# Second feed-forward stage of a two-block transformer kernel: six of its eight 512-feature chunks by seven products of quarters

## The chip, the cores and the metric

The kernel runs on one core of a Trainium2 chip. The time is the device time of one execution in microseconds (us); a comparison uses the median of several executions.

## The reference, cut to what matters

The reference is two transformer blocks in float32 over 512 tokens of width 1024. The first block has two layers: latent attention with a feed-forward stage, then sliding-window attention with a feed-forward stage. The second block has a SwiGLU stage, a dilated attention with pooling, and another SwiGLU stage. What matters here is the feed-forward stage of layer i = 1 and its input:

```python
def modulate(x, g, shift, scale):
    return rmsnorm(x, g) * (1.0 + scale[:, None, :]) + shift[:, None, :]
...
h = modulate(x, g_mlp[i], sh2, sc2)                               # x, h: (1, 512, 1024)
y = jnp.square(jax.nn.relu(h @ w_ff1[i])) @ w_ff2[i]              # 1024 -> 4096 -> 1024
x = x + gt2[:, None, :] * y
```

## The kernel before, in words

Everything is kept transposed: a tile has 128 features on the partitions and the 512 tokens along the row. Every float32 product is made of three matmuls (`mm3`): each operand is split into a rounded high part and the low rest, and high x high, high x low and low x high are summed in PSUM. ScalarE makes the high part of a weight (`act_hi`), VectorE the low part (`dve_lo`), and the same two engines make the parts of the activations.

**Weights.** `PLAN` and `WT` list all weights in the order of use. A weight of 1024 KB (128 partitions x 2048 elements) goes by a DMA of SyncE into one of three `RAW` buffers; its parts go into `WHI` and `WLO`, which have room for three such weights, or for six tiles of 1024 elements (names `UH`, `UL`). `AHEAD[w]` is the last weight that can be prepared while w is in use; `act_split` and `dve_split` prepare up to a given one. Both engines work through one list each, in the order in which the code was written: whatever stands ahead is done first.

**A feed-forward stage** (`pe_ff`, `act_ff`, `dve_ff`) has four blocks q of 1024 hidden features. The up-projection of block q + 1 stands ahead of the down-projection of block q. A chunk of 512 features takes two weights, 96 matmuls of 512 columns. Of the first chunk the tokens come in two halves of 256 columns (`halves`). A hidden tile goes PSUM, ReLU on ScalarE, square on VectorE, high part on ScalarE, low part on VectorE (`act_up`, `dve_up`). A down-projection is added to `X` by VectorE (`dve_resid`, `dve_add_x`). The stage begins with an opening (`act_opening`, `dve_opening`) that finishes the normalization of its input, and the last down-projection of a stage carries the sums of squares for the next one.

**The SwiGLU stages** (`pe_glu`, `act_glu`, `dve_glu`) already have both forms. Their first 768 features are computed plainly (`pe_gate`), the other 2048 in chunks of 512 by `pe_unit`. A unit takes seven products, m = 0 to 6, of a 512 x 256 quarter of weights (or a sum of quarters) and 256 tokens (or a sum of quarters of h). A product is 2 x 4 x 3 = 24 matmuls of 256 columns, so a unit has 168. It uses three PSUM banks: x, y and z. Between products, partial results are copied out (`act_keep`) and joined with later ones (`dve_join`). TensorE waits in the code for three things of these: product 2 waits until product 0's result was copied (`copied, (u, 1)`), product 3 until product 1's was, product 4 until product 2's was. VectorE makes the sums of weight quarters (`dve_sum`, products 1 to 4) and the four sums of h (`dve_t_sum`), which are made once for a stage and split by `act_t_hi` and `dve_t_lo`. In `dve_lo_seven` the sum for tile m + 1 is made just ahead of the low part of tile m. For the sums of h the stage keeps its h before the split in `H32`.

The rows of the profile name the helper lines: L66 matmul, L72 activation, L75 tensor_tensor, L83 scalar_tensor_tensor, L101 dma_start. In the ordinary chunks of the second feed-forward stage a row "DVE L75 128x2048 fp32r" is a low part of a weight; in a unit "DVE L75 t<-t,PS 128x512" is a join.

Of the kernel before, what the change touches and what calls it, by code (L numbers as in the profile page):

```python
# [4 lines left out]
S = 512  # L5
# [141 lines left out]
def bass_two_blocks(nc, A, out):  # L147
    ctx = ExitStack()
    with ctx:
# [352 lines left out]
        def count(name):  # L502
# [1169 lines left out]
        def norm_of(N, T, gain, shift, mods, h_free, before):  # L1672
# [10 lines left out]
        n_glu1 = norm_of("glu1", ("down", 1, 3), lambda j: G2[:, j:j + 1], None, [(misc, "g2")],  # L1683
                         lambda hf: [(acc, (("up", 1, 3, 1), 3, F))], [(acc, ("sum", "ff1", 1))])
        n_mix = norm_of("mix", ("w2", 1, 3), lambda j: col("mix_norm", j), None, [],
# [3 lines left out]
        n_end = norm_of("end", ("w2", 2, 3), None, None, [], None, [(acc, ("used", WX["s2"][-1] + 6))])  # L1689
        n_glu1.update(h32=H32[0])  # L1690
        n_glu2.update(h32=H32[1])

# [596 lines left out]
        def g_unit(i, c, gate):  # L2289
            return WX[f"s{i}"][2 * (c - 2) + gate]  # L2290

# [16 lines left out]
        def quarter_h(buf, r, t):  # L2308
            return buf[:, 4 * r:4 * r + 4, 256 * t:256 * t + 256]

        def dve_t_sum(e, i, n, N):
            h = H32[i - 1]
            e.wait_ge(hmul, (N, 7, 1))
            if n == 1:
                e.tensor_tensor(TL32[0][:, :, :], quarter_h(h, 0, 1), quarter_h(h, 0, 0), ALU.subtract).then_inc(
                    t_sum, (i, 1))
            elif n == 2:
                e.wait_ge(t_sum, (i, 1))
                e.tensor_tensor(TL32[1][:, :, :], quarter_h(h, 1, 1), TL32[0][:, :, :], ALU.subtract).then_inc(
                    t_sum, (i, 2))  # L2320
            else:
                if i == 1:
                    e.wait_ge(x_up, ("first", 7))
                e.tensor_tensor(TL32[2][:, :, :], quarter_h(h, 1, 1), quarter_h(h, 0, 1), ALU.subtract).then_inc(
                    t_sum, (i, 3))
                b21 = quarter_h(h, 1, 0)
                e.wait_ge(t_sum, (i, 2))
                e.wait_ge(h_lo, (N, 6, 0))
                e.wait_ge(h_lo_pool, (N, 7, 0))
                e.tensor_tensor(b21, b21, TL32[1][:, :, :], ALU.subtract).then_inc(t_sum, (i, 4))  # L2330

        def act_t_hi(e, i, n):
            if n < 4:
                e.wait_ge(t_sum, (i, n))
                e.activation(TH[n - 1][:, :, :], TL32[n - 1][:, :, :], ACT.Copy).then_inc(t_hi, (i, n))
            else:
                e.wait_ge(t_sum, (i, 4))
                e.wait_ge(acc, ("used", g_ws(i, 2)[1]))
                e.activation(quarter_h(HHI, 0, 1), quarter_h(H32[i - 1], 1, 0), ACT.Copy).then_inc(t_hi, (i, 4))

        def dve_t_lo(e, i, n):
            e.wait_ge(t_hi, (i, n))
            if n == 1:
                e.wait_ge(t_sum, (i, 2))
            if n == 2:
                e.wait_ge(t_sum, (i, 4))
            if n < 4:
                e.tensor_tensor(TL[n - 1][:, :, :], TL32[n - 1][:, :, :], TH[n - 1][:, :, :].bitcast(F32),
                                ALU.subtract).then_inc(t_lo, (i, n))
            else:  # L2350
                e.tensor_tensor(quarter_h(HLO, 0, 1), quarter_h(H32[i - 1], 1, 0), quarter_h(HHI, 0, 1).bitcast(F32),
                                ALU.subtract).then_inc(t_lo, (i, 4))
# [62 lines left out]
        def pe_unit(e, i, c, gate, nm):  # L2415
# [21 lines left out]
            def of_h(r, t):  # L2437
                for k in range(4 * r, 4 * r + 4):
                    e.wait_ge(h_hi, (nm["N"], k, t))
                    e.wait_ge(h_lo_pool if k % 2 else h_lo, (nm["N"], k, t))  # L2440
                return quarter_h(HHI, r, t), quarter_h(HLO, r, t)
# [84 lines left out]
        def dve_low(e, u, q):  # L2526
            i, c, gate = u
            if gate:
# [5 lines left out]
        def dve_unit(e, i, c, gate, nm):  # L2534
            u, w0 = (i, c, gate), g_unit(i, c, gate)
            dve_split(e, AHEAD[w0] - 1)
            dve_split(e, AHEAD[w0 + 1] - 1)
            dve_split(e, AHEAD[w0 + 2] - 1)
            dve_split(e, AHEAD[w0 + 3] - 1)
# [12 lines left out]
            dve_low(e, u, Q22)  # L2552
            dve_low(e, u, Q11)
            dve_times(e, u, Q21)
            dve_low(e, u, Q21)

# [91 lines left out]
        def pool_glu_norm(e, nm):  # L2648
            pool_normed(e, nm, 0, UPPER)
            pool_normed(e, nm, 1, ALL)  # L2650


# [595 lines left out]
        def pe_program(e):  # L3248
# [5 lines left out]
            pe_swa(e)  # L3254
            pe_ff(e, 1, n_ff1, n_glu1)
            pe_glu(e, 1, n_glu1, n_mix)
# [4 lines left out]
        def act_program(e):  # L3261
# [7 lines left out]
            act_swa(e)  # L3269
            act_ff(e, 1, n_ff1, n_glu1)  # L3270
            act_glu(e, 1, n_glu1, n_mix)
# [4 lines left out]
        def dve_program(e):  # L3276
# [6 lines left out]
            dve_swa(e)  # L3283
            dve_ff(e, 1, n_ff1, n_glu1, lambda j, h: (x_up, ("so", j, h)))
            dve_glu(e, 1, n_glu1, n_mix, lambda j, h: (x_up, ("first", j)))
# [125 lines left out]
```

## Time and profile before

| | |
|---|---|
| median of 3 executions | 2292.75 us (2289.44 to 2293.8) |
| the profiled execution | 2297.01 us, span of its instructions 2295.2 us |
| TensorE matmul busy | 2209.9 us, 96% of the span |
| VectorE busy | 1363.3 us, 59% |
| ScalarE busy | 916.4 us, 40% |
| GpSimd busy | 180.7 us, 8% |
| mean granted TensorE clock | 0.983 of full speed |
| second feed-forward stage | about 829 to 1188 us from the start of the span |

Busy times are unions of intervals on an engine; a matmul's end is modelled, and its own duration (hundreds of ns) overlaps its neighbours. The rate of TensorE is therefore read from how far apart the results of equal pieces of work arrive on the other engines.

### The profile page before, as it was taken

Reading aid. Unit: us, or ns where it says so; the run is one execution under the profiler, and the core shown is the slowest. Engines: PE = TensorE matmul, PEld = TensorE weight load, DVE = VectorE, ACT = ScalarE, POOL = GpSimd, SP = SyncE. Lnnn points to the kernel's source line nnn. Section 1 sums busy time; section 2 is a strip of 40 time slices with the busy share of each in tenths; the row PEclk is TensorE's granted clock in tenths of the full one; section 3 lists DMA queues with packets and bytes.
Section 4 is the critical chain, followed back from the end, with each engine's and each line's share of the span. In section 5 each row is a group of like instructions: output and inputs, shape, how many; then the busy total and the mean of one; then the engine's idle time right before and its main releaser. Section 6 shows DMA issues by size and latency. Waiting matters only on the chain.

```text
span 2295.2 us, 30850 instructions
## 1 busy us (share of the span) xinstructions
PE 2209.9 (96%) x12811; PEld 1930.2 (84%) x12811; DVE 1363.3 (59%) x2069; ACT 916.4 (40%) x1377; POOL 180.7 (8%) x155
## 2 busy tenths in 40 slices
PE   5989999999999899999999999999999999999998
PEld 3877888888898798888898999997878889899997
DVE  5677566556576664343356667754564545666674
ACT  3556343223255643232243444434443333433442
POOL 7220000000032100000020000002012001000000
PEclk8999999999999999999999999999999999999999
DMA  6442244555430213322312333333211332133230
GB/s 232 142 140 83 92 155 176 184 184 203 173 108 20 74 56 113 107 92 92 103 64 70 105 102 102 102 101 109 64 38 66 115 104 74 65 120 101 94 117 38
DMA packets 127728, 245.64 MB, mean 107 GB/s; under 512 B 4763, under 2 KB 36854, under 8 KB 127462
## 3 DMA queue, kind: packets, MB, share of 16 engines
q1 hardware_dynamic: 122832, 228.02, 29.4%
q0 software_dynamic: 4096, 15.28, 2.0%
q8 instruction: 102, 1.67, 0.3%
q10 hardware_dynamic: 662, 0.37, 0.1%
q14 instruction: 36, 0.29, 0.0%
HBM read 241.56 MB, written 2.10 MB: 106 GB/s over the span
## 4 chain that ended last, share of the span: by engine, by line
PE 83%; DVE 9%; ACT 3%; DMA 2%; issue 2%; POOL 0%; SPq 0%; DVEq 0%; ACTq 0%
PE PS L66 82%; DVE t L75 4%; ACT t L72 3%; DVE t L83 2%; DVE t L86 1%; DMA t<-in_ffn_w_dram 1%; PE PS L69 1%; DMA t<-in_w_ada_dram 1%; DVE t L79 0%; POOL t L75 0%; DVE t L92 0%; DVE t L80 0%; SPq L101 0%; DVE t L95 0%; DVEq L58 0%
## 5 line engine op out<-in xcount | busy, mean ns | idle before, releaser
L66 PE MATMUL PS<-t,t 128*128 128x256 f32 (+3 forms) x12444 | 2159.5, 337 | 54.0 <-ACT t L72 15.2
L66 PEld LDWEIGHTS PS<-t,t 128*128 128x128 f32 (+1 forms) x12444 | 1885.9, 190 | 324.7 <-issue 60.6
L72 ACT ACTIVATE t<-t 128x2048 fp32r<-128x2048 f32 (+8 forms) x663 | 605.9, 930 | 1000.8 <-DVE t L75 410.5
L75 DVE TENSOR_TENSOR t<-t,t 128x512 fp32r<-128x512 f32 (+9 forms) x640 | 730.4, 1155 | 450.1 <-ACT t L72 427.8
L72 ACT ACTIVATE t<-PS 128x512 f32<-128x512 f32 (+4 forms) x331 | 177.5, 551 | 244.1 <-PE PS L66 181.2
L75 POOL TENSOR_TENSOR t<-t,t 128x512 f32<-128x512 f32 (+2 forms) x71 | 86.6, 1220 | 1125.6 <-ACT t L72 952.3
L75 DVE TENSOR_TENSOR t<-t,PS 128x512 f32<-128x512 f32 (+2 forms) x116 | 70.9, 616 | 139.8 <-PE PS L66 134.3
L83 DVE SCALAR_TENSOR_TENSOR t<-t,t,t 128x1024 f32<-128x1024 f32 (+2 forms) x149 | 139.9, 943 | 16.8 <-DMA t<-in_w_ada_dram 11.1
L72 ACT ACTIVATE t<-t,t 128x256 fp32r<-128x256 f32 (+5 forms) x212 | 112.4, 537 | 91.1 <-DVE t L83 46.0
L83 DVE SCALAR_TENSOR_TENSOR t<-PS,t,t 128x512 f32<-128x512 f32 (+3 forms) x120 | 76.8, 642 | 95.7 <-PE PS L66 85.7
L75 DVE TENSOR_TENSOR t<-t 128x512 f32<-128x512 f32 (+4 forms) x119 | 80.9, 680 | 23.7 <-ACT t L72 23.0
L69 PE MATMUL PS<-t,t 128*128 128x128 f32 (+1 forms) x367 | 60.0, 305 | 27.0 <-DMA t<-in_x_dram 6.9
L83 DVE SCALAR_TENSOR_TENSOR t<-PS,t 128x512 f32<-128x512 f32 (+1 forms) x84 | 49.3, 610 | 53.5 <-PE PS L66 53.5
L69 PEld LDWEIGHTS PS<-t,t 128*128 128x128 f32 (+1 forms) x367 | 46.5, 155 | 35.8 <-issue 10.6
L83 DVE SCALAR_TENSOR_TENSOR t<-t,t,PS 128x256 f32<-128x256 f32 (+1 forms) x133 | 60.9, 487 | 20.6 <-PE PS L66 17.1
L79 DVE TENSOR_SCALAR t<-t,t 128x128 f32<-128x128 f32 (+5 forms) x159 | 56.7, 389 | 5.4 <-DMA t<-in_w_ada_dram 3.1
L79 POOL TENSOR_SCALAR t<-t 128x512 f32<-128x512 f32 x28 | 48.9, 1748 | 73.5 <-DVE t L86 49.2
L86 DVE CUSTOM_DVE_ANT_0 t<-PS,t 128x128 f32<-128x128 f32 (+1 forms) x112 | 38.4, 352 | 20.7 <-PE PS L66 20.6
L75 DVE TENSOR_TENSOR t<-PS,t 128x512 fp32r<-128x512 f32 (+2 forms) x40 | 24.9, 634 | 34.1 <-ACT t L72 24.2
L101 POOL DMA_DIRECT2D t<-in_k_dist_dram x1 | 0.5, 543 | 426.3 <-PE PS L66 426.3
L72 ACT ACTIVATE t<-PS,t 128x2 f32<-128x2 f32 (+3 forms) x44 | 19.0, 432 | 29.9 <-PE PS L66 29.2
L86 DVE CUSTOM_DVE_ANT_0 t<-PS,t,t 128x384 f32<-128x384 f32 (+3 forms) x56 | 29.2, 522 | 2.0
(30 smaller groups left out, 154.1 us busy)
## 6 DMA issues: line engine op xcount, KB each, us to landing
t<-in_w_ff_dram SPq DMA_DIRECT2D x64, 1024.0 KB, 5.2
t<-in_ffn_w_dram SPq DMA_DIRECT2D x60, 1024.0 KB, 4.9
t<-in_w_ada_dram SPq DMA_DIRECT2D x36, 1024.0 KB, 5.6
t<-in_w_in_dram SPq DMA_DIRECT2D x13, 1024.0 KB, 4.9
t<-in_w_ada_dram POOLq DMA_DIRECT2D x24, 512.0 KB, 4.3
t<-in_swa_w_qkv_dram SPq DMA_DIRECT2D x6, 1024.0 KB, 5.4
t<-in_ffn_w_dram SPq DMA_DIRECT2D x8, 768.0 KB, 4.4
t<-in_w_in_dram SPq DMA_DIRECT2D x24, 256.0 KB, 3.7
```

The lines of the kernel that those rows point to most:

```text
L66: return Instr(self.real and self.real.matmul(o, lhs, rhs, start=start, stop=stop, **more))
L69: return Instr(self.real and self.real.transpose(o, src, ident))
L72: return Instr(self.real and self.real.activation(o, src, func, **more))
L75: return Instr(self.real and self.real.tensor_tensor(o, a, b, op))
L79: return Instr(self.real and self.real.tensor_scalar(o, a, s1, s2, op0))
L83: return Instr(self.real and self.real.scalar_tensor_tensor(o, a, s, b, op0, op1))
L86: return Instr(self.real and self.real.tensor_tensor_reduce(**more))
L101: return Instr(self.real and self.real.dma_start(o, src))
```

## The change

The second feed-forward stage gets functions of its own, `pe_ff1`, `act_ff1` and `dve_ff1`. Of its 4096 hidden features the first 1024 (chunks c = 0 and 1) are computed plainly, the other six chunks (c = 2 to 7) by `pe_unit`. The order on TensorE is: chunks 0 and 1, unit 2, down-projection 0, units 3 and 4, down 1, units 5 and 6, down 2, unit 7, down 3. A down-projection q uses chunks 2q and 2q + 1. The unit's activation becomes three operations of ScalarE on each quarter of 128 x 512 (ReLU, square, high part); VectorE makes the low parts, two of the four of a unit later than before (`dve_late`). Since this stage's h has a shift (`sh2`), two of the four sums of h add it when they are split, as four pieces of 256 columns each. h before the split goes to `H32[0]`. The four sums of h and their parts are made while chunks 0 and 1 are computed. Parts of the diff (the pure renaming of `H32` indices and the calls in the four programs are left out):

```diff
+        def ff1_plan():
+            w1, w2 = wt(A["w_ff1"][1]), wt(A["w_ff2"][1])
+            square("up1", w1)
+            for q, chunks in enumerate(FUNITS):
+                for c in chunks:
+                    unit("s0", w1, 512 * c)
+                square("down1", w2, k0=8 * q)
+
+        FUNITS = ((2,), (3, 4), (5, 6), (7,))
...
         def act_t_hi(e, i, n):
             if n < 4:
                 e.wait_ge(t_sum, (i, n))
+                if i == 0 and n > 1:
+                    for k in range(4):
+                        e.activation(TH[n - 1][:, k, :], TL32[n - 1][:, k, :], ACT.Identity, bias=t_shift(n, k)).then_inc(
+                            t_hi, (i, n))
+                    return
...
-            e.activation(quarter_of(GL32[s], q), src, ACT.Silu).then_inc(relu, (u, q))
+            g = quarter_of(GL32[s], q)
+            if i:
+                e.activation(g, src, ACT.Silu).then_inc(relu, (u, q))
+                return
+            e.activation(g, src, ACT.Relu).then_inc(relu, (u, q))
+            e.wait_ge(relu, (u, q))
+            e.activation(g, g, ACT.Square).then_inc(squared, (u, q))
+            e.wait_ge(squared, (u, q))
+            e.activation(quarter_of(GH[s], q), g, ACT.Copy).then_inc(hid_hi, (u, q))
...
+        def act_ff1(e, nm, nxt):
+            ws = WX["up1"]
+            act_opening(e, nm, ws[0:2])
+            act_step(e, ws[0])
+            act_up1(e, 0, 0)
+            act_up1(e, 0, 1)
+            act_step(e, ws[2])
+            act_t_hi(e, 0, 1)
+            act_t_hi(e, 0, 2)
+            act_step(e, ws[3])
+            act_t_hi(e, 0, 3)
+            act_up1(e, 1, F)
+            for q in range(4):
+                for c in FUNITS[q]:
+                    act_unit(e, 0, c, 0)
...
+        def dve_ff1(e, nm, nxt, before):
+            ws = WX["up1"]
+            dve_opening(e, nm, ws[0:2])
+            dve_step(e, ws[0])
+            dve_up1(e, 0, 0)
+            dve_t_sum(e, 0, 1, "ff1")
+            dve_t_sum(e, 0, 2, "ff1")
+            dve_up1(e, 0, 1)
+            dve_step(e, ws[2])
+            dve_t_sum(e, 0, 3, "ff1")
+            dve_t_lo(e, 0, 1)
+            dve_t_lo(e, 0, 2)
+            dve_step(e, ws[3])
+            dve_t_lo(e, 0, 3)
+            dve_up1(e, 1, F)
+            for q in range(4):
+                late = None
+                for c in FUNITS[q]:
+                    dve_unit(e, 0, c, 0, nm, late)
+                    late = (0, c, 0)
+                dve_late(e, late)
```

**Place A, ScalarE between the first chunk and unit 2.** Before, ScalarE comes from the last tiles of chunk 0 (`t_125<-`, the high parts), makes the high parts of three weights and goes on with the four tiles of chunk 1 (`<-PS 128x512` is the ReLU, then the high part):

```order
L72 ACTIVATE t_125<-t_61 128x256
L72 ACTIVATE t_54<-t_51 128x2048
L72 ACTIVATE t_52<-t_49 128x2048
L72 ACTIVATE t_53<-t_50 128x2048
L72 ACTIVATE t_62<-PS 128x512
L72 ACTIVATE t_125<-t_62 128x512
L72 ACTIVATE t_63<-PS 128x512
```

Now, at the same place (t_150 to t_155 are the unit's weight tiles, t_163 to t_165 the sums that VectorE made for them, t_141 to t_143 the high parts of the sums of h, which are t_147 to t_149):

```order
L72 ACTIVATE t_130<-t_61 128x256
L72 ACTIVATE t_54<-t_51 128x2048
L72 ACTIVATE t_150<-t_49 128x1024
L72 ACTIVATE t_151<-t_163 128x1024
L72 ACTIVATE t_141<-t_147 128x1024
L72 ACTIVATE t_142<-t_148,t_78 128x256 x4
L72 ACTIVATE t_152<-t_164 128x1024
L72 ACTIVATE t_153<-t_165 128x1024
L72 ACTIVATE t_143<-t_149,t_82 128x256 x4
L72 ACTIVATE t_62<-PS 128x512
L72 ACTIVATE t_131<-t_62 128x512
```

Four weight tiles and three sums of h stand ahead of the first ReLU of chunk 1. And behind the last tile of chunk 1 the list goes on with tile m = 4 and then with the copy of product 0 of unit 2 (`t_63<-PS`), tile 5, and the copies of products 1 and 2:

```order
L72 ACTIVATE t_62<-PS 128x512
L72 ACTIVATE t_131<-t_62 128x512
L72 ACTIVATE t_154<-t_166 128x1024
L72 ACTIVATE t_63<-PS 128x512
L72 ACTIVATE t_155<-t_50 128x1024
L72 ACTIVATE t_61<-PS 128x512
L72 ACTIVATE t_62<-PS 128x512
```

The copy of product 0 moved behind all of chunk 1's tiles.

**Place B, VectorE over the same stretch,** from the second sum of h to the third. It begins behind the tiles of chunk 0's second half; t_57 is the low part of the fourth plain weight, t_156 to t_158 those of tiles 0 to 2:

```order
L75 TENSOR_TENSOR t_57<-t_51,t_54 128x2048
L75 TENSOR_TENSOR t_163<-t_49,t_50 128x1024
L75 TENSOR_TENSOR t_156<-t_49,t_150 128x1024
L75 TENSOR_TENSOR t_82<-t_78 128x4
L75 TENSOR_TENSOR t_149<-t_138 128x1024
L75 TENSOR_TENSOR t_138<-t_138,t_148 128x4x256
L75 TENSOR_TENSOR t_144<-t_147,t_141 128x1024
L83 SCALAR_TENSOR_TENSOR t_145<-t_148,t_78,t_142 128x256 x4
L75 TENSOR_TENSOR t_164<-t_163,t_49 128x1024
L75 TENSOR_TENSOR t_157<-t_163,t_151 128x1024
L75 TENSOR_TENSOR t_165<-t_50,t_164 128x1024
L75 TENSOR_TENSOR t_158<-t_164,t_152 128x1024
```

Before, two low parts of plain weights stood here and nothing else.

**Place C, ScalarE at the end of unit 2** (the same in unit 7). t_62, t_61 and t_63 are the joined quarters; t_53 is the high part of the first weight of the down-projection that follows the unit:

```order
L72 ACTIVATE t_135<-t_62 128x2x256
L72 ACTIVATE t_135<-t_135 128x2x256
L72 ACTIVATE t_129<-t_135 128x2x256
L72 ACTIVATE t_135<-t_61 128x2x256
L72 ACTIVATE t_135<-t_135 128x2x256
L72 ACTIVATE t_129<-t_135 128x2x256
L72 ACTIVATE t_53<-t_51 128x2048
L72 ACTIVATE t_135<-t_63 128x2x256
```

That weight stands behind two quarters of three operations each.

## Rows read from the trace of the kernel before

**Rows 1.** The page: span, TensorE's busy time, and the chain that ended last.

```profile
span 2295.2 us, 30850 instructions
...
PE 2209.9 (96%) x12811; PEld 1930.2 (84%) x12811; DVE 1363.3 (59%) x2069; ACT 916.4 (40%) x1377; POOL 180.7 (8%) x155
...
PE 83%; DVE 9%; ACT 3%; DMA 2%; issue 2%; POOL 0%; SPq 0%; DVEq 0%; ACTq 0%
```

**Rows 2.** Timeline of TensorE: start, us, instruction, count, idle before and its releaser.

```profile
849.68 339.29 PE L66 MATMUL PS<-t,t 128*128 128x256 f32 x1628 [1.43 <-ACT t L72]
```

**Rows 3.** Timeline of VectorE, plain chunks: low parts of every second weight.

```profile
935.30 2.29 DVE L75 TENSOR_TENSOR t<-t,t 128x2048 fp32r<-128x2048 f32 x1 [6.71 <-ACT t L72]
...
957.06 2.29 DVE L75 TENSOR_TENSOR t<-t,t 128x2048 fp32r<-128x2048 f32 x1 [8.59 <-ACT t L72]
```

**Rows 4.** Timeline of VectorE in a unit of the first SwiGLU stage: two joins.

```profile
1345.06 0.69 DVE L75 TENSOR_TENSOR t<-t,PS 128x512 f32<-128x512 f32 x1 [5.84 <-PE PS L66]
...
1347.94 0.69 DVE L75 TENSOR_TENSOR t<-t,PS 128x512 f32<-128x512 f32 x1 [1.05 <-PE PS L66]
```

**Rows 5.** Timeline of VectorE, chunk 0 and chunk 1 of the second feed-forward stage.

```profile
851.87 0.43 DVE L75 TENSOR_TENSOR t<-t,t 128x256 fp32r<-128x256 f32 x1 [0.48 <-ACT t L72]
...
853.12 0.43 DVE L75 TENSOR_TENSOR t<-t,t 128x256 fp32r<-128x256 f32 x1 [0.48 <-ACT t L72]
853.46 0.42 DVE L75 TENSOR_TENSOR t<-t 128x256 f32<-128x256 f32 x1
...
872.23 0.68 DVE L75 TENSOR_TENSOR t<-t 128x512 f32<-128x512 f32 x1
...
874.22 0.68 DVE L75 TENSOR_TENSOR t<-t 128x512 f32<-128x512 f32 x1
```

**Rows 6.** Timeline of ScalarE, last tile of chunk 0, two tiles and last tile of chunk 1.

```profile
857.16 0.38 ACT L72 ACTIVATE t<-PS 128x256 f32<-128x256 f32 x1
...
872.95 0.63 ACT L72 ACTIVATE t<-t 128x512 fp32r<-128x512 f32 x1 [1.56 <-DVE t L75]
...
878.95 0.60 ACT L72 ACTIVATE t<-PS 128x512 f32<-128x512 f32 x1 [0.73 <-DVE t L75]
```

**Rows 7.** Groups of instructions by form, whole run: count, busy us, mean ns, idle before.

```profile
L75 DVE TENSOR_TENSOR t<-t,t 128x2048 fp32r<-128x2048 f32 x127 | 290.9, 2296 | 275.9 <-ACT t L72 275.8
L72 ACT ACTIVATE t<-t 128x2048 fp32r<-128x2048 f32 x127 | 241.6, 1909 | 382.3 <-PE PS L66 380.0 <-DMA t<-in_mla_w_ukv_dram 1.9
L75 DVE TENSOR_TENSOR t<-t,t 128x1024 fp32r<-128x1024 f32 x122 | 148.6, 1222 | 25.2 <-ACT t L72 21.1
L72 ACT ACTIVATE t<-t 128x1024 fp32r<-128x1024 f32 x122 | 128.4, 1056 | 146.7 <-DVE t L75 146.5
L83 DVE SCALAR_TENSOR_TENSOR t<-t,t,t 128x256 fp32r<-128x256 f32 x64 | 31.9, 499 | 4.0 <-ACT t L72 4.0
L72 ACT ACTIVATE t<-t,t 128x256 fp32r<-128x256 f32 x64 | 31.4, 507 | 46.0 <-DVE t L83 46.0
```

**Rows 8.** Timeline of ScalarE in a SwiGLU unit: quarters taken after a join.

```profile
1345.78 2.44 ACT L72 ACTIVATE t<-t 128x512 f32<-128x512 f32 x2 [2.06 <-DVE t L75]
```

**Rows 9.** Timeline of TensorE: one of its longest idle stretches inside the program.

```profile
215.25 3.54 PE L66 MATMUL PS<-t,t 128*128 128x1 f32 x16 [3.90 <-DVE t L83]
```

**Rows 10.** Windows: PE, PEld, DVE, ACT, POOL busy, then PEclk, DMA share, GB/s.

```profile
215.00:222.00 7.00, 6.75 (x28) 6.27 (x29) 3.24 (x7) 1.97 (x4) 0.00 (x0) 0.52 0.00 0
...
1603.00:1611.00 8.00, 5.83 (x27) 4.36 (x28) 5.09 (x7) 4.44 (x7) 2.30 (x2) 1.00 0.34 98
```

**Rows 11.** Timeline of VectorE where two SwiGLU units stand behind each other.

```profile
1469.91 2.36 DVE L75 TENSOR_TENSOR t<-t,t 128x1024 f32<-128x1024 f32 x2 [2.27 <-DMA t<-in_ffn_w_dram]
1472.19 0.68 DVE L75 TENSOR_TENSOR t<-t,PS 128x512 f32<-128x512 f32 x1
```

**Rows 12.** Timeline of ScalarE, same stretch: product 2 copied, then the next unit's product 0.

```profile
1467.24 0.60 ACT L72 ACTIVATE t<-PS 128x512 f32<-128x512 f32 x1 [0.85 <-PE PS L66]
...
1482.04 0.60 ACT L72 ACTIVATE t<-PS 128x512 f32<-128x512 f32 x1 [0.82 <-PE PS L66]
```

More of the change, by code:

```diff
@@ L526, in bass_two_blocks @@
         misc, misc_act, misc_pool = count("small_dve"), count("small_act"), count("small_pool")
+        squared = count("squared_act")
         summed, t_sum, t_hi, t_lo, joined = (count(n) for n in (
@@ L2346, in dve_t_lo @@
                 e.wait_ge(t_sum, (i, 4))
-            if n < 4:
+            if i == 0 and n in (2, 3):
+                for k in range(4):
+                    e.scalar_tensor_tensor(TL[n - 1][:, k, :], TL32[n - 1][:, k, :], t_shift(n, k),
+                                           TH[n - 1][:, k, :].bitcast(F32), ALU.add, ALU.subtract).then_inc(t_lo, (i, n))
+            elif n < 4:
                 e.tensor_tensor(TL[n - 1][:, :, :], TL32[n - 1][:, :, :], TH[n - 1][:, :, :].bitcast(F32),
@@ L2439, in of_h @@
                     e.wait_ge(h_hi, (nm["N"], k, t))
[L2440 removed]
+                    e.wait_ge(h_lo_pool if nm["shift"] is None and k % 2 else h_lo, (nm["N"], k, t))
                 return quarter_h(HHI, r, t), quarter_h(HLO, r, t)
@@ L2532, in dve_low, with dve_late, dve_unit @@
                                 ALU.subtract).then_inc(hid_lo, (u, q))
-        def dve_unit(e, i, c, gate, nm):
+        def dve_late(e, u):
+            dve_low(e, u, Q11)
+            dve_low(e, u, Q21)
+        def dve_unit(e, i, c, gate, nm, late=None):
             u, w0 = (i, c, gate), g_unit(i, c, gate)
@@ L2537, in dve_unit @@
             dve_split(e, AHEAD[w0 + 1] - 1)
+            if late:
+                dve_late(e, late)
             dve_split(e, AHEAD[w0 + 2] - 1)
@@ L2552, in dve_unit @@
             dve_low(e, u, Q22)
-            dve_low(e, u, Q11)
-            dve_times(e, u, Q21)
-            dve_low(e, u, Q21)
+            if i:
+                dve_low(e, u, Q11)
+                dve_times(e, u, Q21)
+                dve_low(e, u, Q21)
         def g_of(i, blk):
@@ L2650, in pool_glu_norm, with pe_up1, act_up1 @@
             pool_normed(e, nm, 1, ALL)
+        def pe_up1(e, c, nm):
+            tag = ("up", 1, c)
+            pe_linear(e, tag, WX["up1"][2 * c:2 * c + 2], FOUR, h_of(nm), lambda n, hf: (relu, (tag, n, hf)), halves=c == 0,
+                      mid=pe_open(e, nm) if c == 0 else None)
+        def act_up1(e, c, hf):
+            s = g_slot(0, c)
+            for n in range(4):
+                key = (("up", 1, c), n, hf)
+                ta.take(key, (hid_lo, key))
+                tm = TMP[ta[key]][:, COLS[hf]]
+                e.wait_ge(acc, key)
+                e.wait_for(ta.free(key))
+                e.activation(tm, PS[:, banks[key], COLS[hf]], ACT.Relu).then_inc(relu, key)
+                e.wait_ge(sqr, key)
+                e.activation(GH[s][:, n, COLS[hf]], tm, ACT.Copy).then_inc(hid_hi, key)
@@ new lines, in pe_ff1 @@
+        def pe_ff1(e, nm, nxt):
+            pe_up1(e, 0, nm)
+            pe_up1(e, 1, nm)
+            for q in range(4):
+                for c in FUNITS[q]:
+                    pe_unit(e, 0, c, 0, nm)
+                for n2 in range(2):
+                    last = q == 3 and n2 == 1
+                    pe_linear(e, (("down", 1, q), n2), down_ws(1, q, n2), FOUR, f_of(q), x_until(("down", 1, q), 4 * n2),
+                              halves=last, mid=pe_close(e, nxt) if last else None)
+        def act_ff1(e, nm, nxt):
[13 more added lines that the diff above has]
+                    act_unit(e, 0, c, 0)
+                for n2 in range(2):
+                    act_resid(e, ("down", 1, q), nxt if q == 3 else None, 4 * n2, down_ws(1, q, n2),
+                              halves=q == 3 and n2 == 1, weighted=True)
@@ new lines, in dve_ff1 @@
+        def dve_ff1(e, nm, nxt, before):
[13 more added lines that the diff above has]
+            dve_up1(e, 1, F)
+            for q in range(4):
+                late = None
+                for c in FUNITS[q]:
+                    dve_unit(e, 0, c, 0, nm, late)
+                    late = (0, c, 0)
+                dve_late(e, late)
+                for n2 in range(2):
+                    T = ("down", 1, q)
+                    dve_resid(e, T, nxt if q == 3 else None, (T, n2), 4 * n2, down_ws(1, q, n2),
+                              lambda j: MOD[:, 1, 40 + j:41 + j],
+                              before if q == 0 else lambda j, h: (x_up, (("down", 1, q - 1), j, h)), [(mod, (1, 5))],
+                              halves=q == 3 and n2 == 1)
```

63 lines of the change are left out of this document (46 added, 17 removed).

## The prediction

> **What bounds the kernel now.** I read the page first [rows 1]: TensorE is busy 96% of the span and has 83% of the chain that ended last. So a change is worth what it does to TensorE's work and to its waits. The timeline of TensorE comes next [rows 2]: from 849.68 us it runs 339 us without a gap, through nearly all of the stage that is changed. Every matmul less there is time gained, and every new wait is time lost. What a matmul costs I read from how far apart equal results arrive on other engines.
>
> **The matmuls.** In plain chunks VectorE makes a weight's low part in step with TensorE: a chunk (two weights, 96 matmuls of 512 columns) lasts 957.06 - 935.30 = 21.76 us, 226.7 ns for a matmul [rows 3]. In a unit the joins of products 3 and 4 are 1347.94 - 1345.06 = 2.88 us apart, 24 matmuls of 256 columns, 120 ns for one [rows 4]. Seven products are 20.16 us. A chunk saves 1.60 us; six save **9.6 us** (576 matmuls of 512 columns, 130.6 us, become 1008 of 256, 121.0 us). An eighth of the columns is saved, but 256 columns cost more than half of 512, so under a half of that eighth is left.
>
> The Trainium skill ("TensorE: Matmul & The Clock Gate", "Wait — 56ns, not 53.3ns?") gives a warm matmul as its columns at 2.4 GHz plus about 2.5 ns. By that the chunk would go from 20.7 to 18.3 us and the six would save 14.2 us. The rows above do not show these spacings for either size, so the sum uses the rows.
>
> **The opening: does ScalarE copy product 0 in time?** This is place A of the change. TensorE finishes chunk 0 at 857.1 (the last ReLU starts at 857.16) and chunk 1 at 878.9 (ReLU at 878.95) [rows 6]. Unit 2's products 0 and 1 then run to 878.9 + 5.76 = 884.7, and product 2 needs the copy of product 0. Before, ScalarE followed TensorE tile by tile. I carry the two lists forward from where they are as before, the end of chunk 0's first half on VectorE at 853.5 [rows 5], with the durations of [rows 7]: 1.2 us for a 1024-element operation of VectorE, 1.06 on ScalarE, 2.29 and 1.91 for 2048 elements, 0.40 to 0.50 for a 256-column piece.
> - VectorE: two sums of h, to 855.9. Four tiles of chunk 0's second half, 1.25 us apart [rows 5], to 861.0.
> - ScalarE: high part of the fourth plain weight, 860.5 to 862.4. VectorE: its low part, to 864.7. TensorE wants it at 857.1 + 10.9 = 868.0: no wait.
> - VectorE: weight sum 1, low part of tile 0, sums 3 and 4 of h, low part of sum 1 of h, five operations and a tiny one, to 870.5. Then four pieces, to 872.1. Then sum 2, low part 1, sum 3, low part 2 (to 876.9).
> - ScalarE, held back by those sums: tile 3 to 876.7, then sum 3 of h in four pieces to 878.3. VectorE: its low part, to 880.0.
> - Chunk 1's four tiles, which were ready from 868.0 + 2.7 = 870.7, start here. One takes 1.99 us (square to square) [rows 5], the high part comes 0.72 after the square [rows 6]. The last square is at 885.9, its high part ends at 887.2, its low part at 887.9.
> - VectorE: weight sum 4, to 889.1. ScalarE: tile 4, to 890.2, and only then the copy, **890.7**.
>
> Product 2 therefore waits 890.7 - 884.7 = **6.0 us**. Nothing hides this: TensorE has no other work in its list. Once it resumes, the later copies and tiles (3 at about 890.2, 4 at 891.4) are ready before their products. Beyond this place the sums of h cost nothing more: they are made once.
>
> **The clock after that wait.** After an idle 3.9 us [rows 9] the granted clock was 0.52 over the next 7 us [rows 10], its lower level of 1.2 GHz nearly throughout; after about 2.2 idle us in another stretch it stayed at 1.00. Six us are longer than both, so I expect the fall. Matmuls then take about 213 ns instead of 120 (256 columns at 1.2 GHz). The low stretch after the restart lasts between 4 and 7 us, which loses 44% of it, 1.8 to 3.1 us. I take **2.3**; no fall would be 0.
>
> **The first weight of the down-projection behind a single unit (place C).** Its high part stands behind the quarter of the second join. A quarter was one operation on ScalarE (0.63 us, with the 2048 high part 2.44 together, 0.72 behind the join [rows 4, 8]); now it is three, 2.0 us. From the join of product 4: 0.72 + 2.0 - 0.1 until the high part starts, + 1.9, + 2.3 for the low part is 6.8 us, while TensorE ends the unit 5.76 us after that join, or a little earlier by its own clock. That is a wait of 1.1 to 1.3 us behind unit 2 and behind unit 7, **2.4 together**. In the pairs the buffers fall the other way: the weight is prepared one product earlier, and nothing waits.
>
> **The pairs.** A unit needs 11 operations of 1024 elements (1.2 us), three joins and four low parts (0.69 us) from VectorE: 18.0 of 20.16 us. ScalarE has 7 x 1.06 + 3 x 0.6 + 4 x 2.0 = 17.2. Both fit, with a lead of several tiles from the down-projection, which asks two low parts and four additions of VectorE in 21.8 us. The tight point is again the copy of product 0 of the second unit. By the same bookkeeping it is done 1.8 us before it is wanted. Where two SwiGLU units stand behind each other, VectorE lost 2.27 us to a DMA [rows 11], and the next unit's product 0 came 14.80 us after product 2 instead of 14.40 [rows 12], so 0.4 us is what such a place cost. I take 0, with 0 to 0.8 for both pairs.
>
> DMA bytes do not change, nor do GpSimd's and SyncE's lists. More ReLU, square and copy on ScalarE in place of squares on VectorE costs nothing by itself. The handover to the SwiGLU stage keeps its instructions: 0.
>
> **Sum.** -9.6 + 6.0 + 2.3 + 2.4 = **+1.1 us**. Against the profiled execution (2297.0, which is 4.3 us or 0.2% above the median of the three) that is 2298.1; against the median of 2292.75 it is 2293.9, and this is what I predict. The bounds: with the 2.4 alone 2285.6; all costs at their upper end (6.0 + 1, 3.1, 2.6, 0.8) 2296.7. About 0.2%, 4.6 us, is what a measurement of this kernel can tell from no change.
>
> **Rivals.**
> - *The opening is not late.* If ScalarE or VectorE gets through the list 6 us sooner than I add up (the sums of h overlap waits that I count twice), the 6.0 and 2.3 go: -7.2, **2285.6**. For it: the SwiGLU stages hide the same sums of h without a wait at their first unit. Against it: they have three plain steps of 21.8 us for this, here there are two, and the list is short of 6 us, not of one. Half of it, a wait under 3 us with no fall of the clock, gives about -4.6 and decides whether it can be measured. Chance 0.22.
> - *The pairs run dry.* The takes of quarters Q11 and Q21 (four us of ScalarE together at the end of a unit) stand ahead of the next unit's first copy. If each of the twelve operations of a unit costs 0.15 us more than I take, or the DMA comes as late as in [rows 11], the margin of 1.8 us is gone. From there each us is paid on TensorE in both pairs, and the weight behind the pair comes late as well: 2 x (1.5 to 2.5) more, +4 to +6, so with the rest **2298 to 2300**, slower. Against it: the bookkeeping and the 0.4 us. Chance 0.13.
> - *Narrow matmuls cost half.* If 256 columns took half of 226.7 ns here, 113.4, the saving would be 16.3 us and the sum about -5: 2287.5. Joins 2.88 us apart speak against it. This is the place of the skill's rule above, by whose figures the sum would be -3.5. Chance 0.03.
> - *The change saves nothing in matmuls* because the units run at another rate: excluded by 168 against 96 in the code and [rows 3, 4].
>
> **How the numbers follow.** Forecast 0.62, not late 0.22, pairs 0.13, narrow 0.03. Two thirds of "not late" and the narrow case are faster by over 0.2%, and a tail of the forecast: 0.21. The pairs and a longer low clock are slower: 0.16. Within 0.2%: 0.63. The range reaches from the middle of "not late" to the pairs: 2285 to 2298.5.
>
> **What would show it.** In the profile after: a TensorE idle stretch of about 6 us some 56 us after the stage's start (near 885), released by ScalarE, and a granted clock near 0.5 behind it; idle stretches of about 1.2 us at the ends of units 2 and 7 released by VectorE; joins 2.88 us apart in the pairs; the stage's end about 1 us later than before. A gap under 3 us at 885 would make the forecast wrong towards faster; idle stretches at product 2 of units 4 and 6 towards slower.

## The result and the profile after

The changed kernel takes 2296.07 us (median, 2293.52 to 2300.51), the kernel before 2293.02 us beside it (2288.96 to 2297.56), 22 runs of each. The ratio is 1.0015, with a 95% interval of 1.0008 to 1.0021: the change costs 1.8 to 4.8 us. The median is inside the predicted range and 0.13% above the kernel before, less than the 0.2% that was named as the bound of "no change" (the upper end of the interval, 4.8 us, just passes it); the sign is the one of the sum.

The page of the changed kernel, the lines that answer to [rows 1]: 432 matmuls more, TensorE 5.9 us less busy, and the span 1.4 us longer all the same.

```profile
span 2296.6 us, 31886 instructions
...
PE 2204.0 (96%) x13243; PEld 1943.2 (85%) x13243; DVE 1415.2 (62%) x2132; ACT 965.9 (42%) x1459; POOL 179.3 (8%) x155
```

The timeline of TensorE over the changed stage, which answers to [rows 2] (start, us, instruction, count, then the idle time before it and what ended it):

```profile
847.39 35.00 PE L66 MATMUL PS<-t,t 128*128 128x256 f32 x204 [1.17 <-ACT t L72]
888.38 17.21 PE L66 MATMUL PS<-t,t 128*128 128x256 f32 x120 [6.00 <-ACT t L72]
906.79 231.66 PE L66 MATMUL PS<-t,t 128*128 128x512 f32 x1416 [1.20 <-issue]
1139.64 49.20 PE L66 MATMUL PS<-t,t 128*128 128x512 f32 x320 [1.20 <-issue]
1189.72 70.46 PE L66 MATMUL PS<-t,t 128*128 128x256 f32 x391 [0.88 <-DVE t L75]
```

Where one stretch of 339 us stood, there are four now. The first row is chunks 0 and 1 and unit 2's products 0 and 1; behind it TensorE waits 6.00 us for ScalarE. The two waits of 1.20 us stand behind unit 2 and behind unit 7. (The releaser reads "issue" and not VectorE, as the prediction had it. VectorE's low part of the weight begins at 904.40 and takes 2.29 us, so it ends 0.1 us before the restart; experiment 4 shows that this weight is what TensorE waits for.) Between 906.79 and the next wait, through both pairs, the view shows no gap.

I measure the stage from TensorE's restart at its head to its restart behind its end: before from 849.68 [rows 2] to 1189.84, now from 847.39 to 1189.72. The first of these ends is this row of the kernel before, from the same view:

```profile
1189.84 1.89 PE L66 MATMUL PS<-t,t 128*128 128x256 f32 x9 [0.88 <-DVE t L75]
```

So 340.16 us became 342.33, **+2.17 us**. This leaves out the opening ahead of the head, which the change touches too. The last point where both kernels still do the same is the start of a run of 370 matmuls, here in the kernel before and in the changed one:

```profile
780.23 53.70 PE L66 MATMUL PS<-t,t 128*64 128x128 f32 x370
...
778.92 53.70 PE L66 MATMUL PS<-t,t 128*64 128x128 f32 x370
```

From there to the head are 849.68 - 780.23 = 69.45 us before and 847.39 - 778.92 = 68.47 now. The opening became 0.98 us shorter, and it is 68.44 to 68.46 us in the other kernels below except that of experiment 2. VectorE and ScalarE finish a tile of h each 0.79 us there instead of each 0.91; that it comes from `H32[0]`, where h now has a place of its own, is likely and was not tested. So from the common point the change costs **+1.19 us**, and +2.17 from head to end.

A stage's length is steadier than the span. From a point of the SwiGLU stage (1464.00 us in the changed kernel) all kernels of this study have the same instructions, and yet the rest of their profiled runs lasted between 828 and 836 us, so a span can differ by some us with no edit at all.

ScalarE's timeline shows why product 2 waited. Chunk 1's last tile, tile m = 4, then the copy of product 0:

```profile
882.81 0.58 ACT L72 ACTIVATE t<-PS 128x512 f32<-128x512 f32 x1
...
886.79 1.06 ACT L72 ACTIVATE t<-t 128x1024 fp32r<-128x1024 f32 x1 [1.89 <-DVE t L75]
887.75 0.58 ACT L72 ACTIVATE t<-PS 128x512 f32<-128x512 f32 x1
```

The copy starts at 887.75, and product 2 at 888.38, which is 41.0 us behind the head of the stage; the bookkeeping had 890.7 - 849.7 = 41.0. It stands behind tiles that ScalarE shares with VectorE in turns, one each 1.99 us.

The clock in windows of 2 us (TensorE busy with its count, granted clock, DMA share, GB/s):

```profile
886.00:888.00 2.00, 0.00 (x0) 0.86 0.00 0
888.00:890.00 2.00, 1.62 (x7) 0.50 0.04 8
...
892.00:894.00 2.00, 2.00 (x11) 0.50 0.78 283
894.00:896.00 2.00, 2.00 (x18) 0.93 0.06 23
```

It falls while TensorE still waits and stays at half, 1.2 GHz, until about 894. The price comes from VectorE's timeline:

```profile
899.88 0.69 DVE L75 TENSOR_TENSOR t<-t,PS 128x512 f32<-128x512 f32 x1 [1.06 <-PE PS L66]
...
923.42 0.75 DVE L83 SCALAR_TENSOR_TENSOR t<-PS,t,t 128x512 f32<-128x512 f32 x1 [0.54 <-PE PS L66]
```

The first row is the join of product 4. It comes 899.88 - 888.38 = 11.50 us after product 2 began; in experiment 3, where the clock stays at 1.00, the same join comes 8.92 us after it (3 x 2.88 = 8.64, and 0.28 by which a join starts behind its product's end). So the fall cost **2.58 us**. The second row is one of the additions of a down-projection. The same addition of the next down-projection, two units later, is at 1007.28:

```profile
1007.28 0.75 DVE L83 SCALAR_TENSOR_TENSOR t<-PS,t,t 128x512 f32<-128x512 f32 x1 [0.53 <-PE PS L66]
```

The step is 83.86 us; a down-projection (192 matmuls at 226.7 ns) and two units of 20.16 us make 83.84. The pair costs nothing beyond its matmuls.

### The profile page after: what moved, and what is told of

Read it like the earlier page. It is cut to its first block, busy times and chain, and to the rows that moved or that the text cites. A ratio compares the mean times of both kernels' runs of the same rounds, so it can differ in the third digit from the quotient of the medians.

```text
span 2296.6 us, 31886 instructions
## 1 busy us (share of the span) xinstructions
PE 2204.0 (96%) x13243; PEld 1943.2 (85%) x13243; DVE 1415.2 (62%) x2132; ACT 965.9 (42%) x1459; POOL 179.3 (8%) x155
## 3 DMA queue, kind: packets, MB, share of 16 engines
q0 software_dynamic: 4096, 15.28, 2.0%
## 4 chain that ended last, share of the span: by engine, by line
PE 81%; DVE 10%; ACT 4%; DMA 2%; issue 2%; POOL 0%; SPq 0%; DVEq 0%; ACTq 0%
PE PS L66 80%; DVE t L75 5%; ACT t L72 4%; DVE t L83 3%; DVE t L86 1%; DMA t<-in_ffn_w_dram 1%; PE PS L69 1%; DMA t<-in_w_ada_dram 1%; DVE t L79 1%; POOL t L75 0%; DVE t L92 0%; DVE t L80 0%; SPq L101 0%; DVE t L95 0%; DVEq L58 0%
## 5 line engine op out<-in xcount | busy, mean ns | idle before, releaser
L66 PE MATMUL PS<-t,t 128*128 128x256 f32 (+4 forms) x12876 | 2152.7, 330 | 62.6 <-ACT t L72 20.9
L66 PEld LDWEIGHTS PS<-t,t 128*128 128x128 f32 (+2 forms) x12876 | 1898.4, 190 | 314.0 <-issue 63.0
L72 ACT ACTIVATE t<-t 128x512 f32<-128x512 f32 (+8 forms) x737 | 655.0, 905 | 954.0 <-DVE t L75 479.2
L75 DVE TENSOR_TENSOR t<-t,t 128x1024 fp32r<-128x1024 f32 (+9 forms) x692 | 776.3, 1138 | 395.4 <-ACT t L72 341.5
L75 DVE TENSOR_TENSOR t<-t,PS 128x512 f32<-128x512 f32 (+2 forms) x134 | 83.3, 626 | 157.3 <-PE PS L66 150.5
L83 DVE SCALAR_TENSOR_TENSOR t<-t,t,t 128x1024 f32<-128x1024 f32 (+2 forms) x157 | 144.8, 929 | 14.5 <-DMA t<-in_w_ada_dram 7.5
L75 DVE TENSOR_TENSOR t<-t 128x512 f32<-128x512 f32 (+4 forms) x104 | 74.2, 714 | 14.9 <-ACT t L72 14.5
L69 PEld LDWEIGHTS PS<-t,t 128*128 128x128 f32 (+1 forms) x367 | 46.9, 156 | 35.1 <-issue 10.4
```

Source lines behind the costliest of these rows:

```text
L66: return Instr(self.real and self.real.matmul(o, lhs, rhs, start=start, stop=stop, **more))
L69: return Instr(self.real and self.real.transpose(o, src, ident))
L72: return Instr(self.real and self.real.activation(o, src, func, **more))
L75: return Instr(self.real and self.real.tensor_tensor(o, a, b, op))
L83: return Instr(self.real and self.real.scalar_tensor_tensor(o, a, s, b, op0, op1))
```

## The experiments

None of them changes what the kernel computes. Each stage length is read from one profiled execution. Medians of the kernel before beside them: 2293.96 us (30 runs) for experiments 1 to 4, 2293.55 us (21 runs) for 5 and 6.

**1. All units in pairs, the first down-projection ahead of them.** Down-projection 0 needs chunks 0 and 1 alone, so it can come before the first unit. It gives ScalarE and VectorE 43.5 us in which TensorE needs little of them, and no unit stands alone in front of a down-projection.

```diff
-        FUNITS = ((2,), (3, 4), (5, 6), (7,))
+        FUNITS = ((), (2, 3), (4, 5), (6, 7))
...
-                dve_late(e, late)
+                if late:
+                    dve_late(e, late)
```

> The order of units becomes: chunks 0 and 1, down-projection 0, units 2 and 3, down 1, units 4 and 5, down 2, units 6 and 7, down 3. All the work stays. Theory: the waits come from where the units stand. The 6.0 us wait at product 2 of the first unit goes, because a down-projection of 43.5 us now lies between the sums of h and that unit; with it the stretch at the low clock (2.9 us) goes, and both waits of 1.2 us, since no unit stands alone. Against the changed kernel -11 us, about 2285; against the kernel before -8 to -9.5 us, ratio 0.996. Three pairs cost 0.1 to 0.4 us each. Rival (pairs run dry, or the sums of h cost the same elsewhere): an idle stretch of 2 us or more at product 2 of units 3, 5 or 7, or at the first down-projection, which takes chunk 1 late; then 2290 or more.

Measured: 2286.23 us (2278.54 to 2288.86, 7 runs), ratio to the kernel before 0.9963 (0.9949 to 0.9977), which is 5 to 12 us faster. TensorE's timeline:

```profile
845.45 330.27 PE L66 MATMUL PS<-t,t 128*128 128x256 f32 x2060 [1.16 <-ACT t L72]
1176.59 1.90 PE L66 MATMUL PS<-t,t 128*128 128x256 f32 x9 [0.88 <-DVE t L75]
```

The view shows no gap in the stage, which lasts 331.14 us: 11.19 less than in the changed kernel, 9.02 less than before. The three waits and the clock were 6.00 + 2.58 + 1.20 + 1.20 = 10.98. So nearly all that the changed kernel lost went with the place of the units. Of the 9.6 us that the matmuls should save 9.0 are seen. The rest stands in the first pair, here by the same addition of down-projections 0 and 1 on VectorE:

```profile
891.04 0.75 DVE L83 SCALAR_TENSOR_TENSOR t<-PS,t,t 128x512 f32<-128x512 f32 x1 [0.54 <-PE PS L66]
...
975.42 0.75 DVE L83 SCALAR_TENSOR_TENSOR t<-PS,t,t 128x512 f32<-128x512 f32 x1 [0.54 <-PE PS L66]
```

That step is 84.38 us, the next two are 83.86 each. The first pair alone loses 0.5 us, a little above the 0.1 to 0.4 expected for a pair; why was not traced. This kernel beats both others.

**2. The four sums of h on GpSimd.** At place B they are VectorE's, and they delay its weights and with them ScalarE's tiles.

```diff
-            dve_t_sum(e, 0, 1, "ff1")
-            dve_t_sum(e, 0, 2, "ff1")
...
-            dve_t_sum(e, 0, 3, "ff1")
...
+        def pool_t_sums(e):
+            for n in (1, 2, 3):
+                dve_t_sum(e, 0, n, "ff1")
```

> The four sums of h move from VectorE to GpSimd, which is idle there; nothing else is touched. Theory: VectorE's list ahead of chunk 1's tiles is what is late, so four operations of 1.2 us less there shorten the wait at product 2 of unit 2 by 4.9 us, from 6.0 to about 1.1, and an idle stretch of 1.1 us leaves the clock at full speed: another 2.9 us. Against the changed kernel -7 to -8 us, about 2288.5, a little faster than before (ratio 0.998). Rival (ScalarE's list, not VectorE's, sets it): the wait shortens by less than 2 us, the clock still falls, and the time stays within 2 us of the changed kernel's.

Measured: 2297.0 us (2293.78 to 2300.72, 12 runs), ratio 1.0015 (1.0006 to 1.0023): no better than the changed kernel. TensorE's timeline:

```profile
851.33 36.48 PE L66 MATMUL PS<-t,t 128*128 128x256 f32 x204 [5.98 <-ACT t L72]
891.02 16.15 PE L66 MATMUL PS<-t,t 128*128 128x256 f32 x120 [3.21 <-ACT t L72]
```

The wait at product 2 did shrink, from 6.00 to 3.21 us, but little of that is what was hoped for. The stage's first wait grew from 1.17 to 5.98 us, and the clock fell behind it (36.48 us for 204 matmuls that take 35.00), so TensorE itself came 1.48 us later to product 2. Counted from the head of the stage, product 2 starts at 891.02 - 851.33 = 39.69 us instead of 40.99: the two lists gained 1.30 us where 4.9 were expected. By its size that is the rival's answer (under 2 us). It is a lower bound of what the sums cost, since VectorE lost another 1.6 us behind the head (its low part at 851.04 took 2.02 us instead of 0.43). Counted from the common point ahead of the opening (778.05 here) the stage ends 2.45 us later than in the changed kernel. What happened stands in the timelines of GpSimd and VectorE, here in this order:

```profile
840.82 2.59 POOL L75 TENSOR_TENSOR t<-t 128x1024 f32<-128x1024 f32 x1 [79.70 <-DVE t L83]
843.49 2.44 POOL L75 TENSOR_TENSOR t<-t,t 128x1024 f32<-128x1024 f32 x1
845.88 4.39 POOL L75 TENSOR_TENSOR t<-t 128x1024 f32<-128x1024 f32 x1
```

```profile
841.31 2.38 DVE L83 SCALAR_TENSOR_TENSOR t<-t,t,t 128x256 fp32r<-128x256 f32 x1 [0.18 <-ACT t L72]
843.61 4.47 DVE L75 TENSOR_TENSOR t<-t,t 128x2048 fp32r<-128x2048 f32 x1
848.00 2.56 DVE L75 TENSOR_TENSOR t<-t 128x256 f32<-128x256 f32 x1
```

In the changed kernel the same three operations of VectorE take 0.48, 2.29 and 0.42 us. They alternate: VectorE's short one ends at 843.69, 0.3 us behind GpSimd's first sum; its long one is done 2.15 us behind GpSimd's second (845.93), as if it had run only then; GpSimd's third takes 4.39 instead of 2.44, over that same time; and VectorE's next ends at 850.56, 0.3 us behind that (850.27). One holds the other up for whole operations. The Trainium skill ("SBUF — State Buffer", "Who interferes with whom") has this as a rule: an operation of VectorE with two inputs in SBUF and one of GpSimd that reads SBUF exclude each other, and the one that comes second waits. The trace agrees, at both engines. So the sums still cost VectorE time, and at a place where it has none to spare.

**3. The wait filled with unused matmuls.** 44 matmuls of 256 columns into a free bank between products 1 and 2 of unit 2; their results are not used. The wait stays as long, but TensorE is busy in it.

```diff
+            if u == (0, 2, 0):
+                e.wait_for(banks.free((u, "z")))
+                for _ in range(44):
+                    e.matmul(PS[:, banks[u, "z"], 0:256], HHI[:, 4, 0:128], HHI[:, 4, 0:256], start=True, stop=True)
```

> 44 matmuls of 256 columns, whose results nobody uses, are put on TensorE between products 1 and 2 of unit 2, where it waits 6.0 us (44 x 0.12 = 5.3 us). Theory: the clock falls because TensorE is idle; filled, the wait still ends at the same moment, but product 2 and what follows run at full speed. The stretch at 0.50 in the windows behind it is gone, the join of product 3 comes 5.8 us after the wait's end instead of 8.6, and the time is 2.9 us less than the changed kernel's, equal to the kernel before (2293). Rival (the clock falls there anyway, or its fall is hidden under ScalarE's and VectorE's later steps): the same time as the changed kernel, 2296.

Measured: 2291.16 us (2289.6 to 2292.08, 11 runs), ratio 0.9991 (0.9982 to 0.9999). TensorE's timeline:

```profile
881.31 5.44 PE L66 MATMUL PS<-t 128*128 128x256 f32 x44
887.47 14.65 PE L66 MATMUL PS<-t,t 128*128 128x256 f32 x120 [0.71 <-ACT t L72]
```

VectorE's timeline, the join of product 4:

```profile
896.39 0.69 DVE L75 TENSOR_TENSOR t<-t,PS 128x512 f32<-128x512 f32 x1 [1.06 <-PE PS L66]
```

The windows at the place where the clock had been at half:

```profile
888.00:890.00 2.00, 2.00 (x19) 1.00 0.30 30
890.00:892.00 2.00, 2.00 (x19) 1.00 1.01 381
```

Product 2 starts 40.98 us behind the head of the stage (846.49), as in the changed kernel, so the wait is untouched. The clock stays at 1.00, and the stage lasts 339.70 us, 2.63 less. The join of product 4 comes 8.92 us after product 2's start instead of 11.50. Both give the term for the clock by itself, 2.6 us, and work that computes nothing was worth it. Against the changed kernel the median is 4.9 us lower; 2.6 of that is in the stage, and where the rest comes from is not shown.

**4. The down-projection's weight ahead of the quarter (place C).** In units 2 and 7 alone:

```diff
+            if u in ((0, 2, 0), (0, 7, 0)):
+                act_split(e, AHEAD[w0 + 6] - 1)
             act_take(e, u, Q22)
```

> In units 2 and 7 alone ScalarE makes the high part of the next down-projection's first weight ahead of the second quarter (Q22) instead of behind it. Theory: this order alone makes the two waits of 1.2 us at the ends of single units. The high part is then ready 1.65 us after the join of product 4, the low part stands behind the join of product 5 and ends 5.8 us after that of product 4, so 0.1 to 0.3 us of each wait is left. Against the changed kernel -2 us, near what can be measured; the idle stretches in the timeline decide. Rival (VectorE's lows or a late DMA hold the weight): both waits stay at 1.0 us or more.

Measured: 2296.52 us (2293.09 to 2298.95, 10 runs), ratio 1.0014 (1.0005 to 1.0023). TensorE's timeline:

```profile
883.94 16.64 PE L66 MATMUL PS<-t,t 128*128 128x256 f32 x120 [6.00 <-ACT t L72]
900.73 231.66 PE L66 MATMUL PS<-t,t 128*128 128x512 f32 x1416 [0.15 <-issue]
1132.54 49.21 PE L66 MATMUL PS<-t,t 128*128 128x512 f32 x320 [0.15 <-issue]
```

Both waits of 1.20 us are 0.15, from one operation moved past three, so place C is what the prediction took it for. The stage (842.95 to 1182.62, 339.67) is 2.66 us shorter. Of this 2.10 are the two waits. Most of the rest is not from this edit's place at all: behind the same wait of 6.00 us the 120 matmuls took 16.64 us instead of 17.21, because the clock had fallen earlier in the wait (0.50 from 882 on, 2 us ahead of the restart) and was back sooner. The medians do not show the gain: the two ratios differ by 0.0001, with intervals of about 1.5 and 2 us to either side, so a gain of 2.7 us is at the edge of what they allow. That the waits are gone is shown; that the time follows is not.

**5. The copy of product 0 two tiles earlier.** Is it ScalarE's order or the two engines' load that makes the 6.0 us?

```diff
                 e.activation(GH[s][:, n, COLS[hf]], tm, ACT.Copy).then_inc(hid_hi, key)
+                if (c, n) == (1, 1):
+                    act_keep(e, (0, 2, 0), 1, 0, "x", Q11, at=4)
```

> The changed kernel with one instruction of ScalarE moved: the copy of product 0 of unit 2 stands between the second and the third tile of chunk 1 instead of behind the fourth tile and tile m = 4 of the weights, and writes a buffer that is free there (same count of instructions, same work). Theory (it is the place of the copy in the list that makes the 6.0 us wait): product 0 ends near 879.5, the copy runs near 881, product 2 starts without a wait at 882.4 and ends at 885.3; product 3 then waits for the high and low part of its weight tile, made behind chunk 1's tiles at about 888, so 2.3 to 3 us; the clock may stay at 1.00 behind a wait that short; about -3.3 us against the changed kernel from the wait alone, -6.2 if the clock stays up as well. Rival (both engines are simply short of time up to this point, so the order makes no difference): the wait moves to product 3 in full, 6 us, and the time stays as that of the changed kernel.

Measured: 2295.79 us (2291.19 to 2298.59, 11 runs), ratio 1.0006 (0.9997 to 1.0015). TensorE's timeline and clock:

```profile
845.51 37.87 PE L66 MATMUL PS<-t,t 128*128 128x256 f32 x228 [1.16 <-ACT t L72]
887.80 13.28 PE L66 MATMUL PS<-t,t 128*128 128x256 f32 x96 [4.42 <-ACT t L72]
```

```profile
886.00:888.00 2.00, 0.20 (x1) 0.97 0.00 0
888.00:890.00 2.00, 2.00 (x10) 0.50 0.67 113
890.00:892.00 2.00, 2.00 (x14) 0.68 1.04 404
```

228 matmuls pass now before the wait: product 2 did not wait. But product 3 did, for 4.42 us. I had left the copy of product 1 out of the expectation; it starts at 887.17, behind tiles 4 and 5, and ends this wait. The clock fell all the same, which the expectation had left open. The stage lasts 339.65 us, 2.68 less: 1.6 from the shorter wait, and 1.0 because the fall cost 1.5 us here and not 2.6 (13.28 us for the 96 matmuls; with the clock up, in experiment 3, they take 14.65 - 2.88 = 11.77). So the order on ScalarE has a part in the 6.0 us, 1.6 of them by this one operation; whether the copy of product 1, moved as well, would gain more was not tried.

**6. One more ReLU on each quarter.** About 2.6 us more on ScalarE per unit, with the same result.

```diff
             e.activation(g, g, ACT.Square).then_inc(squared, (u, q))
             e.wait_ge(squared, (u, q))
+            e.activation(g, g, ACT.Relu).then_inc(again, (u, q))
+            e.wait_ge(again, (u, q))
```

> The changed kernel with one more ReLU on each quarter of all six units (the result is unchanged): about 0.65 us each, 2.6 us of ScalarE per unit, which takes it from 17.2 to 19.8 of a unit's 20.16 us. It asks how near the pairs are to running dry. Theory (margin 1.2 us before the copy of product 0 of a pair's second unit): two quarters stand ahead of that copy, +1.3 us, so the margin is just used up and TensorE waits 0 to 0.5 us there in each pair; behind units 2 and 7 two quarters stand ahead of the weight's high part, so these waits grow from 1.2 to about 2.5 us each; the stage becomes 2.6 to 3.6 us longer. Rival (the delay adds up from quarter to quarter through the buffers, as in the prediction's case of the pairs that run dry): TensorE waits 1.5 us or more in each pair and behind the pairs too, the stage 5 us or more longer.

Measured: 2300.95 us (2295.04 to 2304.02, 11 runs), ratio 1.0026 (1.0017 to 1.0035). TensorE's timeline:

```profile
887.92 17.19 PE L66 MATMUL PS<-t,t 128*128 128x256 f32 x120 [5.97 <-ACT t L72]
906.96 71.30 PE L66 MATMUL PS<-t,t 128*128 128x512 f32 x408 [1.85 <-issue]
978.55 84.11 PE L66 MATMUL PS<-t,t 128*128 128x256 f32 x528 [0.28 <-ACT t L72]
1063.57 78.35 PE L66 MATMUL PS<-t,t 128*128 128x256 f32 x480 [0.91 <-ACT t L72]
1143.77 49.20 PE L66 MATMUL PS<-t,t 128*128 128x512 f32 x320 [1.86 <-issue]
```

The margin of the pairs is used up as expected: there are waits of 0.28 and 0.91 us at product 2 of the second units. The second is above the 0 to 0.5 expected, and VectorE's timeline shows what differs there, a weight that came later by DMA:

```profile
962.04 2.36 DVE L75 TENSOR_TENSOR t<-t,t 128x1024 f32<-128x1024 f32 x2 [1.10 <-DMA t<-in_w_ff_dram]
...
1047.06 2.36 DVE L75 TENSOR_TENSOR t<-t,t 128x1024 f32<-128x1024 f32 x2 [1.72 <-DMA t<-in_w_ff_dram]
```

VectorE waited 0.62 us longer in the second pair, and TensorE 0.63. In the changed kernel these two waits are 1.22 and 1.09 us. The down-projections are now 84.40 and 85.01 us apart (additions at 925.19, 1009.59 and 1094.60) instead of 83.86, +0.5 and +1.2, and the 0.65 us of the quarters do not add up. The waits behind units 2 and 7 grew by 0.65 us each, one ReLU and not the two that I had counted. The stage is 4.57 us longer, though, above the 2.6 to 3.6 expected, and 1.6 of that stands in none of these. It is the clock behind the wait of 1.85 us:

```profile
907.00:908.00 1.00, 1.00 (x3) 0.69 0.17 27
908.00:909.00 1.00, 1.00 (x4) 0.50 0.48 133
909.00:910.00 1.00, 1.00 (x4) 0.50 1.00 379
...
1144.00:1148.00 4.00, 4.00 (x19) 1.00 0.76 248
```

(From the restart at 906.96 to the addition at 925.19 are 18.23 us; in the changed kernel, where the clock stays at 1.00, 923.42 - 906.79 = 16.63.) The last row is behind the wait of 1.86 us, where it did not fall.

## Why the prediction was right

Its sum was +1.1 us, its time 2293.9. The median came out 2.2 us above the number, at the upper side of the range; the trace says +2.17 from head to end and +1.19 from the common point ahead of the opening. The nearness of +1.19 to +1.1 is partly luck: the sum had neither the 0.98 us that the opening gained nor about as much that the stage lost beyond the terms. The terms themselves were right in place and cause. By its own steps:

- **The matmuls, -9.6.** Right. The stage without a wait (experiment 1) is 9.02 us shorter with 0.5 lost in its first pair, and 83.86 us for a down-projection and a pair is what 226.7 and 120 ns make. A saving of 14.2 or 16.3 us, as in "narrow matmuls cost half", does not fit these numbers. Two slips of working: what is left of the eighth of the columns is 9.6 of 16.3 us, over a half and not under it, and the sum of "narrow matmuls cost half" is -5.6, 2287.2, not about -5.
- **The opening, +6.0.** Right in place, releaser and size: 6.00. The count of the two lists, carried forward from a point where both kernels agree, was exact to 0.1 us over 41. That is not two errors that cancel: chunk 1's tiles started 28.5 us behind the head (875.85) where the count had 28.6. Experiments 2 and 5 give the parts: without the sums of h on VectorE the lists gained 1.30 us (2.9 with what VectorE lost anew), with the copy moved 1.6, so neither alone makes the 6.0. (At place B three low parts of plain weights stood before, with t_57, and not two.)
- **The clock, +2.3.** The mechanism was right and the size near: 2.6, within the bounds of 1.8 to 3.1. I took a value near the middle for a low stretch of 4 to 7 us. It was a little under 6 us after the restart (888.4 to 894 and a part of the next window), and 44% of that is 2.5. Experiment 3 took this term away alone. That it was 2.6 and not 2.0 is chance: behind the same 6.00 us in experiment 4 it was 2.0.
- **The first weight behind a single unit, +2.4.** Right: 1.20 twice, and experiment 4 removes it with one operation moved.
- **The pairs, 0.** Right in the time. The margin of the copy was put at 1.8 us; in the trace of the changed kernel it was 1.2 (rows below). The late DMA of the rival was there, about 1.1 to 1.2 us instead of 2.27, and fitted into the margin.
- **The sum.** With the measured terms -9.6 + 6.0 + 2.6 + 2.4 is +1.4, and the stage has +2.17. The 0.8 that remain are not traced to one place: 0.3 of them stand between the two waits of 1.20 us (231.65 us for 231.36 by the durations used), 0.2 in unit 2 (14.64 us for 14.40 in experiment 3, where the clock stays up). The opening's -0.98 was not in the sum. The median's +3.05 has an interval of 1.8 to 4.8 us, which holds the +2.17 and not the +1.19; where the program spends the difference, these traces do not show.
- **"The opening is not late"** did not happen: VectorE and ScalarE are short by the whole 6 us.

ScalarE's timeline in the first pair, the copies of products 0 and 1 of its second unit:

```profile
974.75 0.58 ACT L72 ACTIVATE t<-PS 128x512 f32<-128x512 f32 x1
...
976.53 0.60 ACT L72 ACTIVATE t<-PS 128x512 f32<-128x512 f32 x1 [0.26 <-PE PS L66]
```

Product 1 was done at 976.5, where product 2 asks for the copy that ended at 975.33. Experiment 6 shows that 0.65 us more on each quarter turns this into waits of 0.3 us, and 0.9 with a later DMA, not the +4 to +6 of "the pairs run dry", which overstated what a us beyond the margin costs.

## What to carry to other kernels

When TensorE has hardly a gap, a cheaper form of the same product is worth its matmuls only if the first use of it comes when the preparing engines are ahead. Here the same six units were 3 us slower or 8 us faster than the plain form, by where one down-projection stood. Before adding up an opening, look for work that already has its inputs and needs nothing from the late engines, and put that first. Where a wait of some us must stay, price the clock behind it as well: behind waits of 6 us it cost 1.5 to 2.6 us more.

## What was not expected of the hardware

- Sums on GpSimd cost VectorE whole operations: 0.48, 2.29 and 0.42 us became 2.38, 4.47 and 2.56 (experiment 2), and the head of the stage came 4.8 us later.
- The length of a wait alone does not tell whether the clock falls. Behind 1.85 us it fell (experiment 6, at 907, some 19 us after the restart from a wait of 5.97), behind 1.86 us in the same run it did not (at 1144), nor behind 1.20 in the changed kernel. Behind 3.21, 4.42 and 6.00 it fell each time. And it fell behind waits of 0.88 and 0.15 us, just after the stage (the row at 1189.84 above), in the kernel before and in the changed one; here before:

```profile
1194.00:1196.00 2.00, 2.00 (x14) 0.72 0.00 0
1196.00:1198.00 2.00, 2.00 (x11) 0.50 0.00 0
```

In experiment 3 it did not fall at that place.
- Nor does the length tell the price. Two waits of 6.00 us cost 2.6 (the changed kernel) and 2.0 us (experiment 4), one of 5.98 us 1.5 (experiment 2), and those of 1.85, 3.21 and 4.42 us 1.5 to 1.6. What decides it stays open.
